# Conditioning weights of an fp32 transformer kernel read in row blocks of 128 by 2048

## What is computed

```python
sc  = jax.nn.silu(c)          # (1, 1024), for the latent stream
scc = jax.nn.silu(c_ctx)      # (1024,),   for the context stream
for l in range(DEPTH):        # two layers
    mod_l = jnp.split(sc  @ ada_w[l] + ada_b[l], 6, axis=-1)   # ada_w[l] is 1024 x 6144
    mod_c = jnp.split(scc @ ada_w[l] + ada_b[l], 6, axis=-1)
    h_lat = _rmsnorm(x_lat, norm_mix[l]) * (1 + mod_l[1]) + mod_l[0]
    h_ctx = _rmsnorm(x_ctx, norm_mix[l]) * (1 + mod_c[1]) + mod_c[0]
    ...
```

## Time and profile before

| what | value |
|---|---|
| median of three runs | 2386.62 us (2386.52 to 2386.75) |
| the profiled execution: span from the first to the last instruction | 2392.7 us |
| PE busy | 2183.2 us, 91% |
| DVE, ACT, POOL busy | 657.4, 356.8, 121.6 us |
| mean granted TensorE clock | 0.964 |
| matmuls of the conditioning (L1306) | 384, busy 51.2 us |
| DMAs of `ada_w` | 48 of 1024 KB |

### The profile page before, as it was taken

The page is one execution under the profiler, slowest core; times in us unless marked ns, Lnnn a source line. Parts: engine busy times, 40 slices in busy tenths (PEclk is TensorE's granted clock), DMA queues, the critical chain, the costliest instruction groups (busy, mean ns, idle before and its releaser), DMA issues. The chain is left out here.

```text
span 2392.7 us, 27727 instructions
## 1 busy us (share of the span) xinstructions
PE 2183.2 (91%) x11542; PEld 1346.1 (56%) x11542; DVE 657.4 (27%) x1482; ACT 356.8 (15%) x830; POOL 121.6 (5%) x164
## 2 busy tenths in 40 slices
PE   6987898999999986999889998897599999989998
PEld 2554664656566543444455554454376458858863
DVE  2143332422222213313531111111455330034201
ACT  2043431200000001112420000000131122011000
POOL 4000000010000001000000000000110000000000
PEclk9998999999999998999989999999899999999999
DMA  9364173799999997521199999999643433443441
GB/s 333 121 222 154 37 280 124 279 420 420 420 420 419 421 420 296 208 70 53 54 362 420 419 420 419 420 419 411 213 153 124 136 106 106 150 141 126 147 154 40
DMA packets 154309, 601.75 MB, mean 252 GB/s; under 512 B 15289, under 2 KB 19073, under 8 KB 103488
## 3 DMA queue, kind: packets, MB, share of 16 engines
q1 hardware_dynamic: 144512, 582.98, 63.1%
q0 software_dynamic: 8144, 11.57, 1.5%
q10 hardware_dynamic: 1520, 5.32, 0.6%
HBM read 589.84 MB, written 21.23 MB: 255 GB/s over the span
## 5 line engine op out<-in xcount | busy, mean ns | idle before, releaser
L366 PE MATMUL psum<-ring,h_t 128*128 128x512 f32 (+1 forms) x1024 | 429.3, 581 | 4.9 <-ACT h_t L1072 2.1
L366 PEld LDWEIGHTS psum<-ring,h_t 128*128 128x128 f32 x1024 | 192.4, 192 | 234.8 <-issue 229.9
L399 PE MATMUL psum<-h_t,ring 128*128 128x256 f32 (+1 forms) x1424 | 311.4, 381 | 4.6 <-ACT ff_hid L2572 2.3
L399 PEld LDWEIGHTS psum<-h_t,ring 128*128 128x128 f32 (+1 forms) x1424 | 270.2, 190 | 45.4 <-issue 3.6
L2386 PE MATMUL psum<-ring,h_t 128*64 128x256 f32 x2272 | 260.4, 382 | 3.1 <-DMA ring<-in_expert_w_dram 2.1
L2386 PEld LDWEIGHTS psum<-ring,h_t 128*64 128x64 f32 x2272 | 158.1, 137 | 88.6 <-issue 11.7
L2386 PE MATMUL psum<-wide,h_t 128*64 128x256 f32 x1664 | 192.7, 385 | 2.3 <-DMA wide<-in_expert_w_dram 1.5
L2386 PEld LDWEIGHTS psum<-wide,h_t 128*64 128x64 f32 x1664 | 115.7, 138 | 67.5 <-issue 9.0
L337 DVE COPY h_t<-psum 128x512 f32<-128x512 f32 (+2 forms) x76 | 50.4, 663 | 317.2 <-PE psum L1940 290.7
L1940 PE MATMUL psum<-gates,h_row_tiles 128*128 128x256 f32 (+1 forms) x512 | 104.8, 359 | 1.4 <-ACT h_row_tiles L337 1.4
L1940 PEld LDWEIGHTS psum<-gates,h_row_tiles 128*128 128x128 f32 x512 | 85.6, 190 | 20.6 <-issue 10.4
(11 more groups left out here) (590 smaller groups left out, 2090.4 us busy)
## 6 DMA issues: line engine op xcount, KB each, us to landing
ring<-in_expert_w_dram SPq DMA_DIRECT2D x210, 1024.0 KB, 24.5
wide<-in_expert_w_dram SPq DMA_DIRECT2D x156, 1024.0 KB, 25.6
ring<-in_ada_w_dram SPq DMA_DIRECT2D x48, 1024.0 KB, 10.8
ring<-in_w_in_dram SPq DMA_DIRECT2D x30, 1024.0 KB, 5.3
ring<-in_diff_w_in_dram SPq DMA_DIRECT2D x12, 1024.0 KB, 16.0
gates<-in_expert_w_dram SPq DMA_DIRECT2D x12, 1024.0 KB, 27.5
x<-in_expert_w_dram SPq DMA_DIRECT2D x12, 1024.0 KB, 28.1
ring<-in_w_gate_dram SPq DMA_DIRECT2D x12, 1024.0 KB, 5.1
```

What stands on the lines that cost most here:

```text
L366: mm = k.nc.tensor.matmul(banks[r][0:m, 0:nn], lhs(k0 + j, r), w[:, j, :], start=(k0 + j == 0), stop=(k0 + j == k_tiles - 1))
L399: mm = k.nc.tensor.matmul(banks[i][0:h, 0:n_rhs], w[:, j, b:b + h], rhs(k0 + j), start=(k0 + j == 0), stop=(k0 + j == k_tiles - 1))
```

## The change

`plan_rows` replaces `plan` for `ada_w`. A chunk is now 128 rows by 2048 columns: partition p holds one row's 2048 numbers, one piece of 8 KB, seen as four blocks of 512. A part is still eight chunks of 1 MB in the same slots. Lane group j now takes column block j of the same 128 rows, and all eight chunks of a part add up in one bank, bank 7; the other groups of the call take turns over banks 0 to 6. At the end of a part ACT copies the bank once, PE transposes it in four pieces, and DVE adds the bias while it reads PSUM. In the first call the groups of `between` are now put behind chunks: the packs behind the fourth, four transposes of `x` behind the sixth and four behind the seventh.

```diff
--- before.py
+++ after.py
@@ -163,6 +163,14 @@
                                     before[-1] if before else None, len(before) + 1))
                 before.append(len(self.chunks) - 1)
 
+    def plan_rows(self, w, n_first):
+
+        for k0 in range(0, D, P):
+            slot = self.next_slot
+            self.next_slot = (slot + 1) % SLOTS
+            self.plan_slot(w[k0:k0 + P, n_first:n_first + 4 * BANK].rearrange("p (j n) -> p j n", n=BANK), (4, BANK),
+                           iter([slot]))
+
     def plan_slot(self, src, shape, slots):
 
         slot = next(slots)
@@ -907,7 +915,7 @@
     sb = k.sb
 
 
-    ada_part = lambda l, part: k.plan(t["ada_w"][l], D, 2 * D, 2 * D * part)
+    ada_part = lambda l, part: k.plan_rows(t["ada_w"][l], 2 * D * part)
     ada_part(0, 0)
     spare = []
     for l in range(2):
@@ -1059,7 +1067,8 @@
                 return copy_by(k, who, h_t[:, kt, :], bank)
             return fill, [(who, raw)]
         pack_group = (turn_packs, [("dve", lambda bank: nc.vector.tensor_copy(cols[:], bank[:, 0:3 * P]))])
-        modulate(0, (0,), {BANK: [pack_group], 2 * BANK: [turn_x(kt) for kt in range(DK)]}, silu_at)
+        modulate(0, (0,), {3: [pack_group], 5: [turn_x(kt) for kt in range(4)], 6: [turn_x(kt) for kt in range(4, DK)]},
+                 silu_at)
         k.need(packs_loaded)
         norm_gains(k, 0, (0,), col, mods, mod_a)
         wait_for(act, now(k.dve_step))
@@ -1234,16 +1243,16 @@
 class Flow:
 
 
-    def __init__(self, k, engines=("pe", "act", "dve", "pool")):
-        self.k, self.at, self.holder, self.seen = k, 0, [None] * 8, {"act": 0, "dve": 0}
+    def __init__(self, k, engines=("pe", "act", "dve", "pool"), turning=8):
+        self.k, self.at, self.holder, self.seen, self.turning = k, 0, [None] * 8, {"act": 0, "dve": 0}, turning
         stage = k.stage()
         for who in engines:
             k.behind(who, stage)
 
-    def group(self, fill, empties, *_, needs=()):
+    def group(self, fill, empties, *_, needs=(), bank=None):
         k = self.k
-        mine = [(self.at + i) % 8 for i in range(len(empties))]
-        self.at += len(empties)
+        mine = [(self.at + i) % self.turning for i in range(len(empties))] if bank is None else [bank]
+        self.at += len(empties) if bank is None else 0
         for sem, n in needs:
 
             k.nc.tensor.wait_ge(sem, n)
@@ -1292,50 +1301,41 @@
 
 
 
+
     nc = k.nc
-    per_part = 6 * D // 3
+    n_blocks = 2 * D // P
     with ExitStack() as tmp:
-        rows = k.sb(f"mod_rows{l}_{parts[0]}", [P, per_part], where=tmp)
-        flow = Flow(k, ("pe", "act", "dve") if started is None else ())
+        rows = k.sb(f"mod_rows{l}_{parts[0]}", [P, BANK], where=tmp)
+        flow = Flow(k, ("pe", "act", "dve") if started is None else (), turning=7)
         wait_for(nc.tensor, started or ())
 
         def product(pe, banks):
-            for k0 in range(0, DK, 4):
+            for kt in range(DK):
                 w = k.take(pe, 4, BANK)
                 for j in range(4):
-                    mm = nc.tensor.matmul(banks[0][32 * j:32 * j + 32, :], silu_c[:, k0 + j, :], w[:, j, :],
-                                          start=(k0 == 0), stop=(k0 + 4 == DK))
+                    mm = nc.tensor.matmul(banks[0][32 * j:32 * j + 32, :], silu_c[:, kt, :], w[:, j, :],
+                                          start=(kt == 0), stop=(kt + 1 == DK))
                 yield mm
                 k.used(k.tensor_done.n)
-
-        def turn(n0, part, copied):
+                flow.groups(between.get(kt, ()))
+
+        def turn(part, copied):
             def fill(pe, banks):
                 for b in range(4):
-                    mm = nc.tensor.transpose(banks[0][:, b * P:(b + 1) * P], rows[:, n0 + b * P:n0 + (b + 1) * P],
-                                             k.ident[:])
+                    mm = nc.tensor.transpose(banks[0][:, b * P:(b + 1) * P], rows[:, b * P:(b + 1) * P], k.ident[:])
                 yield mm
 
-            def add_up(bank):
-                b0 = (part * per_part + n0) // P
-                m = mods[:, l, b0:b0 + 4, :]
-                chain(nc.vector, k.dve_step, nc.vector.tensor_reduce(
-                    m, bank.rearrange("p (b j q) -> p b q j", j=4, q=32)[:, :, 0:2, :], AX.X, ALU.add))
-                wait_for(nc.vector, now(k.dve_evac))
-                return nc.vector.tensor_tensor(m, m, col(f"ada_b{l}", b0, 4).unsqueeze(2).to_broadcast([P, 4, 2]), ALU.add)
-            flow.group(fill, [("dve", add_up)], needs=copied)
-        turn_of = turns()
+            def add_bias(bank):
+                first = part * n_blocks
+                return nc.vector.tensor_tensor(
+                    mods[:, l, first:first + n_blocks, :].rearrange("p (j b) q -> p b j q", j=4),
+                    bank.rearrange("p (b j q) -> p b j q", j=4, q=32)[:, :, :, 0:2],
+                    col(f"ada_b{l}", first, n_blocks).rearrange("p (j b) -> p b j", j=4).unsqueeze(3).to_broadcast(
+                        [P, 4, 4, 2]), ALU.add)
+            flow.group(fill, [("dve", add_bias)], needs=copied)
         for part in parts:
-            copied = {}
-            for n0 in range(0, per_part, BANK):
-                who = next(turn_of)
-                flow.group(product, [(who, lambda bank, who=who, n0=n0: copy_by(k, who, rows[:, n0:n0 + BANK], bank))])
-                copied[n0] = now(k.act_evac if who == "act" else k.dve_evac)
-                flow.groups(between.get(n0, ()))
-                if n0 >= BANK * (2 if between else 1):
-                    turn(n0 - BANK, part, copied[n0 - BANK])
-                if between and n0 == 2 * BANK:
-                    turn(0, part, copied[0])
-            turn(per_part - BANK, part, copied[per_part - BANK])
+            flow.group(product, [("act", lambda bank: nc.scalar.copy(rows[:], bank))], bank=7)
+            turn(part, now(k.act_evac))
         k.holder = flow.holder
         k.pump()
 
```

## The result

Over twelve runs of each on the same chips the changed kernel takes 2382.93 us and the kernel before 2386.68. The ratio is 0.9978, 95% interval 0.9968 to 0.9988: 5.3 us faster, 2.9 to 7.6. (The two medians by themselves lie 3.8 us apart, a ratio of 0.9984, which is inside the interval.) One profiled execution of each gives more, 2383.1 us of span against 2392.7. Single executions scatter: those of the kernel before lie between 2383.05 and 2391.84 us, so one pair of spans settles no microsecond. The stages do.

The account below looks back on a forecast made before the run. Serial PE and tail work bounds the later calls, DMA landing order the first. 2392.7 - 8.8 (five calls) + 1.3 (first call) = 2385.2 us of span, 2379.1 us as a median; range 2374 to 2385.5.

Parts of the forecast that it names:

- The product: Calls two to six: eight chunks in one piece on PE cost 7.08 us, which removes 1.44 us a call.
- The tail: Calls two to six, from the last matmul to the next stage: 1.69 us instead of 2.01, 0.32 less.
- the term of the five calls: Calls two to six: 1.76 us saved in each, 8.8 us together, with bounds of 7.0 and 9.3.
- The turn of one packet each: DMA queues in the first call: engines take one packet per queue in turn; 8 KB pieces lengthen each turn by 0.23 us.
- the identity's term: First call, ACT's queue: nine lengthened turns of 0.23 us after 8.48, so the identity is seen at 10.5 us.
- rival four: First call's queues: turns drain whole chunks, inputs land as late as about 31 us, total 2382.1; chance 0.04.
- Half speed was to last until 31.5: PE in the first call: full clock returns 3.5 us after work resumes at 28.0, so from 31.5 us.
- the first call costs: First call: late inputs move the first projection from 39.48 to 40.8 us, a cost of 1.3 us.
- Rival three: Stages behind the calls: PE's clock takes back 5 us, total 2384.2; chance of 3 us or more lost 0.12.
- Rivals one: First call: small queues are not held up, so it gains 2.5 us, total 2375.3; chance 0.10.
- two: First call: PE stays at half speed throughout, projection at 46.5 us, 7 us later, total 2384.8; chance 0.08.
- five: First call's stream: 8 KB rows 24 KB apart read slowly, near 600 ns a piece, total 2391.4; chance 0.06.

Follow-up runs that it names:

- the second profile: The changed kernel run again without any edit, against the kernel before: ratio 0.9968 (0.9954 to 0.9981), first projection at 40.00 us.
- the old form: First call as in the kernel before, chunks of 512 rows by 512 columns; with the other five calls as changed, ratio 0.9976 to the kernel before.
- `x` first: The changed kernel with x and ctx loaded on SP's queue ahead of the first chunk; ratio to the kernel before 0.9958 in both measurements.

## Why the prediction was right, step by step

**The later calls.** The product was to take 7.08 us and took 7.07. The tail was to take 1.69 us and took 1.91: the copy starts 0.14 us behind the product instead of 0.07, the transposes 0.78 behind it instead of 0.72, DVE 0.79 after their start instead of 0.69, and the next stage 0.34 after the bias instead of 0.28. So the term of the five calls is 7.9 us where the prediction has 8.8; it lay inside the bounds of 7.0 and 9.3. The gain was PE's own work and its place, as the run with the transposes last shows, and not the DMAs.

**The queues.** The identity was forecast for 10.5 us and seen at 9.74, `x` for 25.8 and 25.05, the packs for 28.0 and 26.93, PE's wait at the packs for some nine microseconds and 8.3. The turn of one packet each carried these numbers, and halving `x`'s pieces confirmed it where it would have failed by bytes. All of them came 0.7 to 1.1 us before their forecast, and most of that is the identity's term: it is 1.26 us later than before where nine turns would make 2.1. `x` then lies 6.9 us further behind the identity than before, the 30 turns of 0.23 us. Turns of whole chunks (rival four) would have put the inputs near 31 us; they were not there. The Trainium skill, "DMA: Bandwidth & Descriptors", section "Queues, rings and completion order", has an engine drain a whole packet, typically 9 to 17 descriptors, in a turn; the trace does not agree with that size, if a record is a descriptor: 209, 210 and 208, and 56 against 56 in a single microsecond, 3.5 an engine, where a turn of nine pieces of 8 KB would take nearly three.

**PE behind them.** Half speed was to last until 31.5; the chunks at 27.77 run at half speed and the transposes at 31.15 at full speed. The packs came 1.1 us before their forecast and the transposes 0.85 before theirs (32.0); from there to the end of the product PE took 5.85 us and not 5.45, so the product ended at 37.00 instead of 37.45. The projection was forecast for 40.8 and starts at 40.31, 40.00 in the second profile, so the first call costs 0.5 to 0.8 us and not 1.3 against the profile before. Against all four profiles of the old form (39.48, 39.94, 37.92, 39.42, mean 39.2) the three of the new form (40.31, 40.19, 40.00, mean 40.2) are 1.0 later.

**The sum.** 2385.2 us of span were forecast and 2383.1 measured; 2379.1 us as a median, against 2386.68 x 0.9978 = 2381.4 by the first measurement and 2379.0 by the second (0.9968). The terms from the stages make 7.1 us where the prediction has 7.5: the later calls gave 0.9 less than forecast and the first call cost 0.5 less, so that the sum is nearer than its terms is luck. And "faster by over 0.2%" is borne out by the stages only; both intervals of the ratio reach across 0.998. What the first measurement lacks of that, 1.8 us, is within its interval. No row accounts for it, but the rows show where the noise is: from the start of the sixth call to the end the ten profiles with the new form of that call took between 2057.4 and 2066.8 us, with hardly any difference in code there. Rival three, the clock, is neither shown nor excluded as a lasting loss: the stretch from the end of the third call to the fourth took 20.63 us with the change and 21.75 before, that from the fourth's next stage to the fifth 88.05 and 90.26, that from the end of the fifth to the sixth 20.62 and 22.30. Against that, the stretch from the end of the second call to the third took 37.81 and 36.72, all behind the sixth call 2054.6 and 2053.3, and that from the first projection to the second call 72.08 and 72.02. In this pair of profiles the stretches between the calls gave 2.5 us in all, so 2.5 of the 9.6 us by which the span fell are not shown to be the change's own; over many runs no such gain shows. Rivals one and two fell with the first call's rows, and five with its stream: with `x` first the chunks came 2.49 us apart, eight pieces an engine at 0.31 us, no slower than the expert pieces, and chunk 8 was never waited for in the changed kernel.

What I had not seen is how the first call could be had cheaper. The prediction treats late inputs as its cost and the stream as slack. With `x` first the call is 3.5 to 4.5 us shorter than with the change, and PE then waits for the stream (chunk 6, 25.63). So the stream has little slack once the inputs are early, and the cure is an order, not a size. And rival three, which I gave the calls alone, may touch any change that starts later work earlier: between the second call and the sixth the lead of the two profiles with `x` first shrank by 4.0 and 4.3 us. That the earlier start is the cause is not shown.

## What to carry to other kernels

Where several queues load at once as here, count packets and not bytes: a bulk stream in larger pieces takes a larger share, and the small loads of other queues, their completions included, come later by pieces times the added length of a turn. Put what is needed first on the same queue ahead of the stream, and then make the stream's pieces large. And when a chain of product, copy, transposes and sum ends in a wait, first look at whether work in front of the last product can stand behind it: two thirds of what a later call gained (1.03 of 1.55 us) needed no new layout.

## What the runs showed that I had not expected

- A short handover was longer where the engine had waited long. In the third call ACT's copy starts 0.14 us behind the product after 10.88 us of idling, in the first call 0.07 after 0.88 us; DVE's read starts 0.13 behind the transposes after 8.74 us, 0.03 after 0.45. This was seen in these places only and not tested.
- A further wait that is long fulfilled, in front of one DVE instruction, costs 0.07 us (9.05 against 8.98 us a call, in three calls).
- The start of one and the same code varies between profiles: the old form's first projection lies at 37.92 to 39.94 us, with the first transposes of `x` at full speed at 27.87 in one and not at 28.77 in another. The times of single executions spread with it, 2381.85 to 2397.33 us over 23 runs of the kernel before.
